# Expert blocks of 32 rows on four 32-column tiles, in an encoder layer with 32 experts on one core

## The reference

```
logits = x2 @ w_router + b_router
top_v, top_i = lax.top_k(logits, 4);  gates = softmax(top_v)
# for each expert e and the tokens that chose it:
gu = xb @ w_gate_up[e] + b_gate_up[e]          # 1024 -> 2048
gate = min(gu[:, :1024], 7);  up = clip(gu[:, 1024:], -7, 7)
hid = (up + 1) * gate * sigmoid(1.702 * gate)
y = hid @ w_down[e] + b_down[e]                # 1024 -> 1024
# the token's result: sum over its four experts of gate * y
```

## Time and profile before

| | before |
|---|---|
| median of 3 runs | 2055.57 us (2051.02 to 2067.83) |
| the profiled execution | 2061.79 us |
| its span | 2060.2 us |
| mean granted TensorE clock | 0.887 |
| TensorE busy | 1719.9 us, 83% |
| VectorE, ScalarE, GpSimd busy | 372.7, 337.3, 117.5 us |
| moved by DMA | 510.75 MB, mean 248 GB/s |

### The profile page before, as it was taken

One profiled execution on the slowest core, in us unless ns is written; L12 is line 12 of the kernel. 1 busy time (PEld: TensorE's weight loads), 2 busy tenths in 40 slices (PEclk: granted clock), 3 DMA queues, 4 the chain that ended last, 5 costly groups with the idle time before them and its releaser, 6 DMA issues.

```text
span 2060.2 us, 19415 instructions
## 1 busy us (share of the span) xinstructions
PE 1719.9 (83%) x7088; PEld 789.1 (38%) x7089; DVE 372.7 (18%) x899; ACT 337.3 (16%) x695; POOL 117.5 (6%) x219
## 2 busy tenths in 40 slices
PE   3999978688889998589877999979799987899890
PEld 1666544355556663333222333323233322233330
DVE  1371143322220011511010111101110111011113
ACT  1141254211221000111110111101111110111111
POOL 0021000000000000200000000000000000000003
PEclk9999976766669999599999999998999999999995
DMA  9396200110013344399999879999977999759894
GB/s 306 118 256 196 102 21 0 34 39 2 1 41 123 113 169 156 141 367 405 408 405 402 317 272 403 405 403 413 401 297 267 412 402 399 290 209 403 315 365 137
DMA packets 112324, 510.75 MB, mean 248 GB/s; under 512 B 8513, under 2 KB 12334, under 8 KB 79390
## 3 DMA queue, kind: packets, MB, share of 16 engines
q1 hardware_dynamic: 95790, 454.97, 56.4%
q0 software_dynamic: 16496, 55.29, 9.2%
HBM read 470.95 MB, written 39.28 MB: 248 GB/s over the span
## 4 chain that ended last, share of the span: by engine, by line
PE 65%; DMA 22%; DVE 6%; ACT 3%; issue 3%; SPq 1%; POOL 0%; DVEq 0%; POOLq 0%; ACTq 0%
PE bank L498 31%; DMA ring<-in_w_gate_up 18%; PE bank L826 12%; PE bank L851 10%; PE bank L834 7%; PE bank L502 2%; PE bank L817 2%; DVE r_c L1118 1%; DMA ring<-in_w_down 1%; ACT ring L878 1%; DMA ring<-in_w_in 1%; DVE r_v L1118 1%; DVE r_kv L1115 1%; ACT r_kv L878 1%; DMA y_rows<-r_xt 0%
## 5 line engine op out<-in xcount | busy, mean ns | idle before, releaser
L826 PE MATMUL bank<-ring,r_kv 128*64 128x512 f32 x1872 | 412.9, 593 | 27.2 <-DMA ring<-in_w_gate_up 27.2
L851 PE MATMUL bank<-ring,r_kv 128*64 128x512 f32 x1248 | 315.0, 662 | 27.8 <-ACT r_kv L878 26.8
L498 PE MATMUL bank<-r_xt,ring 128*128 128x336 f32 (+2 forms) x896 | 259.8, 453 | 8.6 <-DMA ring<-in_w_in 8.6
L826 PEld LDWEIGHTS bank<-ring,r_kv 128*64 128x64 f32 x1872 | 131.2, 137 | 302.6 <-issue 253.4
L1112 DVE TENSOR_SCALAR r_kv<-bank 128x512 f32<-128x512 f32 (+1 forms) x80 | 55.0, 687 | 1038.0 <-PE bank L834 1016.2
L498 PEld LDWEIGHTS bank<-r_xt,ring 128*128 128x128 f32 (+2 forms) x896 | 167.5, 188 | 99.1 <-issue 20.4
L834 PE MATMUL bank<-ring,r_kv 128*64 128x512 f32 x624 | 151.3, 630 | 39.9 <-DMA ring<-in_w_gate_up 39.9
L851 PEld LDWEIGHTS bank<-ring,r_kv 128*64 128x64 f32 x1248 | 94.7, 153 | 223.2 <-issue 181.5
L1070 ACT ACTIVATE r_o<-r_kv 128x512 f32<-128x512 f32 x39 | 24.6, 630 | 562.2 <-DVE r_kv L1112 562.2
L502 PE MATMUL bank<-const,r_v 64*128 64x64 f32 (+3 forms) x524 | 62.9, 258 | 60.0 <-DVE r_v L1118 49.3
L834 PEld LDWEIGHTS bank<-ring,r_kv 128*64 128x64 f32 x624 | 45.5, 144 | 141.6 <-issue 88.4
(11 more groups left out here) (212 smaller groups left out, 1092.7 us busy)
## 6 DMA issues: line engine op xcount, KB each, us to landing
ring<-in_w_gate_up SPq DMA_DIRECT2D x128, 2048.0 KB, 20.6
ring<-in_w_down SPq DMA_DIRECT2D x64, 2048.0 KB, 21.4
ring<-in_w_in SPq DMA_DIRECT2D x12, 2048.0 KB, 7.8
r_v<-x_rows POOLq DMA_DIRECT2D x40, 256.0 KB, 7.3
y_rows<-r_xt POOLq DMA_DIRECT2D x78, 128.0 KB, 5.5
x_rows<-r_c POOLq DMA_DIRECT2D x10, 768.0 KB, 18.4
x_rows<-r_c POOLq DMA_DIRECT2D x6, 1024.0 KB, 21.6
y_rows<-r_c POOLq DMA_DIRECT2D x1, 5376.0 KB, 33.1
```

Of the source, the lines that this page charges most:

```text
L498: ins = pe.matmul(out, l, r, start=(n == 0), stop=(n == len(pairs) - 1), **kw)
L826: ins = pe.matmul(half(gate_bank if q < 2 else up_bank, q % 2), xg[:, 2 * c + k, :], w[:, k, 512 * q:512 * q + 512], start=False, stop=Fal ...
L851: ins = pe.matmul(half(out_bank, t), hidT[:, j, BLK * c:BLK * c + BLK], w[:, j, 512 * t:512 * t + 512], start=(c == 0 and j == 0), stop=(c ...
```

## The change

`BLK` goes from 64 to 32, and everything of a block with it. The stationary operand has 32 columns, and four 32-column tiles of the array hold the same rows and produce a quarter of the output columns each, 256 per matmul; each PSUM bank holds 256 columns on 128 partitions. So gate and up are 64 matmuls of 256 columns instead of 32 of 512, down 32 instead of 16, the bias 8 instead of 4. The elementwise work of a block is on 128x256 instead of 128x512 elements, and `hid` is turned in two pieces instead of four.

The weights of an expert come in twelve transfers of 1 MiB (eight for gate and up, four for down) instead of six of 2 MiB; the last two of gate and up are waited for together. The down weights are grouped so that transfer j holds rows of both halves of the hidden dimension.

The turning of the next block's rows stays behind gate and up; the next block's bias matmuls move there too, behind a wait for the clamp of up (`m_read`). TensorE instead of ScalarE waits for `yrow_free`, ahead of the down product. GpSimd stores `yrow` in four pieces instead of two, and loads rows two blocks ahead instead of one.

The row buffers get MAXB = 74 blocks of 32 rows instead of 53 of 64; the tables for blocks grow from 55 to 76 entries, and the counting of blocks (`more`) has nine steps instead of four.

```diff
-NE, TOPK, BLK = 32, 4, 64
+NE, TOPK, BLK = 32, 4, 32
...
-        xg = r3(r_kv[:, 0:512], 8)
-        hidT = r3(r_kv[:, 512:1024], 4)
-        gt = r_kv[:, 1024:1536]
-        up = r_kv[:, 2048:2560]
-        sg = r_o[:, 0:512]
+        xg = r3(r_kv[:, 0:256], 8)
+        hidT = r3(r_kv[:, 512:768], 2)
+        gt = r_kv[:, 1024:1280]
+        up = r_kv[:, 2048:2304]
+        sg = r_o[:, 0:256]
         gateT = r_o[0:NE, 1024:1024 + NT]
-        hid = r_v[:, 0:512]
+        hid = r_v[:, 0:256]
         xrow = r_v[0:BLK, 1216:2240]
-        yrow = r_xt[:, 1280:1792]
-
-        def up_w(c):
-            return ring[:, UPSLOT[c] * SLOT:(UPSLOT[c] + 1) * SLOT].rearrange("p (k f) -> p k f", k=2)
-
-        def dn_w(c):
-            return ring[:, DNSLOT[c] * SLOT:(DNSLOT[c] + 1) * SLOT].rearrange("p (k f) -> p k f", k=4)
+        yrow = r_xt[:, 1280:1536]
+
+        def up_w(k):
+            at = UPSLOT[k // 2] * SLOT + 2 * D * (k % 2)
+            return ring[:, at:at + 2 * D]
+
+        def dn_w(j):
+            at = DNSLOT[j // 2] * SLOT + 2 * D * (j % 2)
+            return ring[:, at:at + 2 * D].rearrange("p (h f) -> p h f", h=2)
...
-            sp.dma_start(dn_w(0), dn[:, 0, 0:4, :]).then_inc(chunk_in[4], 16)
-            sp.dma_start(dn_w(1), dn[:, 0, 4:8, :]).then_inc(chunk_in[5], 16)
+            for j in range(4):
+                sp.dma_start(dn_w(j), dn[:, 0, :, j, :]).then_inc(dn_in[j], 16)
             sp.wait_ge(moe_tab, 1)
             with sp.Fori(1, NE) as e:
                 before = sp.value_load(firsti[0:1, bass.ds(e, 1)].bitcast(I32), min_val=0, max_val=MAXB)
-                for c in range(4):
-                    sp.wait_ge(m_up, before * 4 + c + 1)
-                    sp.dma_start(up_w(c), gu[:, bass.ds(e, 1), 2 * c:2 * c + 2, :].rearrange("p a k f -> p (a k) f")
-                                 ).then_inc(chunk_in[c], 16)
-                for c in range(2):
-                    sp.wait_ge(m_down, before * 2 + c + 1)
-                    sp.dma_start(dn_w(c), dn[:, bass.ds(e, 1), 4 * c:4 * c + 4, :].rearrange("p a k f -> p (a k) f")
-                                 ).then_inc(chunk_in[4 + c], 16)
+                for k in range(8):
+                    sp.wait_ge(m_up, before * 7 + min(k, 6) + 1)
+                    sp.dma_start(up_w(k), gu[:, bass.ds(e, 1), k, :].rearrange("p a f -> p (a f)")
+                                 ).then_inc(up_in[k], 16)
+                for j in range(4):
+                    sp.wait_ge(m_down, before * 4 + j + 1)
+                    sp.dma_start(dn_w(j), dn[:, bass.ds(e, 1), :, j, :].rearrange("p a h f -> p (a h) f")
+                                 ).then_inc(dn_in[j], 16)
...
+            def tile(bank, t):
+                return bank[BLK * t:BLK * t + BLK, 0:256]
+
+            def bias(b):
+
+                pe.wait_ge(m_pick, b + 1)
+                for q in range(8):
+                    pe.matmul(tile(gate_bank if q < 4 else up_bank, q % 4), pick[:, q // 2, :],
+                              bgu[:, 256 * (q % 2):256 * (q % 2) + 256], start=True, stop=False, skip_group_check=True)
+
+            bias(0)
             with pe.Fori(0, nb) as b:
                 e = pe.value_load(bei[0:1, bass.ds(b, 1)].bitcast(I32), min_val=0, max_val=NE - 1)
-
-                def half(bank, t):
-                    return bank[BLK * t:BLK * t + BLK, :]
-
-                pe.wait_ge(m_pick, b + 1)
-                for q in range(4):
-                    pe.matmul(half(gate_bank if q < 2 else up_bank, q % 2), pick[:, q, :], bgu[:, :],
-                              start=True, stop=False, skip_group_check=True)
                 pe.wait_ge(m_xg, b + 1)
-                for c in range(4):
-                    pe.wait_ge(chunk_in[c], 16 * e + 16)
-                    w = up_w(c)
-                    if c < 3:
-                        for k in range(2):
-                            for q in range(4):
-                                ins = pe.matmul(half(gate_bank if q < 2 else up_bank, q % 2), xg[:, 2 * c + k, :],
-                                                w[:, k, 512 * q:512 * q + 512], start=False, stop=False,
-                                                skip_group_check=True)
-                        ins.then_inc(m_up, 1)
-                    else:
-                        for bank_, q0, done in ((gate_bank, 0, m_gate), (up_bank, 2, m_up)):
-                            for k in range(2):
-                                for t in range(2):
-                                    ins = pe.matmul(half(bank_, t), xg[:, 2 * c + k, :],
-                                                    w[:, k, 512 * (q0 + t):512 * (q0 + t) + 512], start=False,
-                                                    stop=(k == 1), skip_group_check=True)
-                            ins.then_inc(done, 1)
+                for k in range(6):
+                    pe.wait_ge(up_in[k], 16 * e + 16)
+                    w = up_w(k)
+                    for q in range(8):
+                        ins = pe.matmul(tile(gate_bank if q < 4 else up_bank, q % 4), xg[:, k, :],
+                                        w[:, 256 * q:256 * q + 256], start=False, stop=False, skip_group_check=True)
+                    ins.then_inc(m_up, 1)
+                for k in (6, 7):
+                    pe.wait_ge(up_in[k], 16 * e + 16)
+                for bank_, q0, done in ((gate_bank, 0, m_gate), (up_bank, 4, m_up)):
+                    for k in (6, 7):
+                        for t in range(4):
+                            ins = pe.matmul(tile(bank_, t), xg[:, k, :],
+                                            up_w(k)[:, 256 * (q0 + t):256 * (q0 + t) + 256], start=False,
+                                            stop=(k == 7), skip_group_check=True)
+                    ins.then_inc(done, 1)
                 pe.wait_ge(m_xrow, 16 * b + 32)
                 pe.sem_inc(m_rows_in, 1)
                 tokens_turned()
+                pe.wait_ge(m_read, b + 1)
+                bias(b + 1)
                 pe.wait_ge(m_hid, b + 1)
-                for j in range(4):
+                for j in range(2):
                     ins = turn(ht_bank[:, 128 * j:128 * j + 128], hid[:, 128 * j:128 * j + 128])
                 ins.then_inc(m_turn, 1)
                 pe.wait_ge(m_hidT, b + 1)
-                for c in range(2):
-                    pe.wait_ge(chunk_in[4 + c], 16 * e + 16)
-                    w = dn_w(c)
-                    for j in range(4):
-                        for t in range(2):
-                            ins = pe.matmul(half(out_bank, t), hidT[:, j, BLK * c:BLK * c + BLK],
-                                            w[:, j, 512 * t:512 * t + 512], start=(c == 0 and j == 0),
-                                            stop=(c == 1 and j == 3), skip_group_check=True)
+                pe.wait_ge(yrow_free, b + 1)
+                for j in range(4):
+                    pe.wait_ge(dn_in[j], 16 * e + 16)
+                    w = dn_w(j)
+                    for h in range(2):
+                        s = 2 * h + j // 2
+                        for t in range(4):
+                            ins = pe.matmul(tile(out_bank, t), hidT[:, j % 2, BLK * s:BLK * s + BLK],
+                                            w[:, h, 256 * t:256 * t + 256], start=(j == 0 and h == 0),
+                                            stop=(j == 3 and h == 1), skip_group_check=True)
                     ins.then_inc(m_down, 1)
...
-                copy(hidT[:, :, :], banks[1][:, :].rearrange("p (j s) -> p j s", j=4)).then_inc(m_hidT, 1)
-                act.wait_ge(m_down, 2 * b + 2)
-                act.wait_ge(yrow_free, b + 1)
-                copy(yrow, banks[4][:, :]).then_inc(m_yrow, 1)
+                copy(hidT[:, :, :], banks[1][:, 0:256].rearrange("p (j s) -> p j s", j=2)).then_inc(m_hidT, 1)
+                act.wait_ge(m_down, 4 * b + 4)
+                copy(yrow, banks[4][:, 0:256]).then_inc(m_yrow, 1)
...
-                ts(gt, banks[2][:, :], LIMIT, ALU.min).then_inc(m_gt, 1)
+                ts(gt, banks[2][:, 0:256], LIMIT, ALU.min).then_inc(m_gt, 1)
                 ts(pick[:, :, :], lane, be[:, bass.ds(dve.snap(b + 1), 1)], ALU.is_equal).then_inc(m_pick, 1)
-                dve.wait_ge(m_up, 4 * b + 4)
-                ts(up, banks[3][:, :], LIMIT, ALU.min, -LIMIT, ALU.max).then_inc(m_dve, 1)
+                dve.wait_ge(m_up, 7 * b + 7)
+                ts(up, banks[3][:, 0:256], LIMIT, ALU.min, -LIMIT, ALU.max).then_inc(m_read, 1)
                 dve.wait_ge(m_sig, b + 1)
                 dve.wait_ge(m_gt, b + 1)
                 tt(gt, gt, sg, ALU.mult).then_inc(m_dve, 1)
-                dve.wait_ge(m_dve, 2 * b + 2)
+                dve.wait_ge(m_read, b + 1)
+                dve.wait_ge(m_dve, b + 1)
                 stt(hid, up, 1.0, gt, ALU.add, ALU.mult).then_inc(m_hid, 1)
...
+            pool.wait_ge(m_gath, 1)
+            pool.dma_start(xrow, x_rows_dram[BLK:2 * BLK, :]).then_inc(m_xrow, 16)
```

(37 more changed lines are left out.)

3 lines of the change are left out of this document (1 added, 2 removed).

## The result

The changed kernel takes 2130.21 us (median of 4 runs, 2127.78 to 2132.54) against 2056.35 us before (2051.02 to 2067.83): ratio 1.0351, 95% interval 1.0306 to 1.0397. It is slower by 74 us; the forecast was 2126 us, 70 slower. The profiled execution has a span of 2129.0 us.

A forecast was written before the change was run, and what follows sets the result against it. The prediction took the DMA queue to bound the loop: first request 877, stream 1005, holes 185 and tail 15 gave 2082 us against 2012, +70. The forecast was 2126 us, range 2078 to 2175.

The forecast's parts named there:

- first request: Start of the expert loop's weight loads: the first weight request stays at 877 us.
- holes: Expert loop: times without a weight request outstanding, behind experts with several blocks; 185 us in all instead of 106.
- a hole behind two blocks: Empty weight queue from an expert's last landing until its second block has used chunk 0; 4.4 us, before 10.9.
- an inner block: Each block beyond an expert's second, run with weights present while nothing is fetched; 13.7 us, before 27.6.
- stream without holes: Expert loop's weight and row transfers: 403.2 MB at 401 GB/s take 1005 us.
- tail behind the last landing: End of the loop: the last expert's second block comes wholly behind the last weight landing; 15 us.
- The DMA queue as the clock of the loop: Expert loop: time without a weight request is lost; faster TensorE gains only there and at the end.
- A block at four tiles: Block's matmuls: four tiles run beside each other, 54 ns an instruction; gate and up 6.9 us, down 3.5.
- yrow_free at TensorE: Down product's wait for the previous block's stores: ready after 8.7 us, needed after 9.2; at slowest landing 0.9 us.
- TensorE as the bound: Rival in the loop: four tiles no better than two, or lower clock; block 23.2 us, up to 2380 us; chance 0.05.
- Smaller transfers: Rival for weight loads: 186 added requests each cost 0.38 us, 71 us more, 2197 us; chance 0.02.
- A faster stream: Rival for weight loads: finer slots raise the rate; at 429 GB/s 2026 us; chance of faster 0.04, within 1% 0.07.

The follow-up runs named there:

- experiment 4: Changed kernel with 32 added float32 matmuls in each block, into PSUM banks that nobody reads; 2174.03 us, ratio 1.0572 to the kernel before.
- experiment 1: Changed kernel with blocks of 64 rows on two 64-column tiles, all else of the change kept; 2022.41 us, ratio 0.9829 to the kernel before.
- experiment 3: Changed kernel with six weight transfers of 2 MB instead of twelve of 1 MB, 32 rows kept; 2164.76 us, ratio 1.0517 to the kernel before.
- experiment 5: Kernel of experiment 1 with weight chunk 6 used when it lands, only chunk 7 waited for at the end; 2012.71 us, ratio 0.9770 to the kernel before.
- experiment 6: Kernel of experiment 1 with the bias matmuls put back to the start of the block; 2063.93 us, ratio 1.0029 to the kernel before.
- experiment 2: Kernel before with only the twelve 1 MB weight transfers instead of six of 2 MB; 2057.94 us, ratio 0.9989 to the kernel before.
- experiment 8: Kernel of experiment 1 with six weight transfers of 2 MB instead of twelve; 2028.29 us, ratio 0.9838 to the kernel before.
- experiment 7: Changed kernel, 32 rows, with weight chunk 6 used when it lands and only chunk 7 waited for; 2134.90 us, ratio 1.0368 to the kernel before.
- experiment 9: Changed kernel, 32 rows, with the bias matmuls put back to the start of the block; 2148.49 us, ratio 1.0429 to the kernel before.

## Why the prediction was right

By its own steps, predicted and measured:

| term | predicted | measured |
|---|---|---|
| first request | 877 | 875.0 |
| holes | 185 | 179 |
| a hole behind two blocks | 4.4 (at full clock 2.8) | 4.1 to 4.6 |
| an inner block | 13.7 (at full clock 12.7) | 13.2 to 13.3 |
| stream without holes | 1005 | 1007 (last weights at 2061.7) |
| tail behind the last landing | 15 | 16 |
| loop ends | 2082 | 2077.8 |
| behind the last down product, more than before | 1 | 3 |

- **Blocks.** 58, as reckoned: the page of the changed kernel counts 232 stores of rows, four for each block. Experts with one block follow each other every 31.0 to 31.3 us, where 31 to 32 were forecast.
- **The DMA queue as the clock of the loop.** Shown by experiment 4 (203 us of matmuls cost 44) and by experiments 1, 3, 5 and 6, in which the time moves with the sum of the holes: 75, 222, 61 and 106 us of holes, 2022, 2165, 2013 and 2064 us. Experiment 2 doesn't speak against it: its holes didn't shrink either. The eleven profiles cut into four parts say the same (us; "stream" is the time from the first to the last weight packet of the loop, less the holes):

| kernel | first packet | stream | holes | behind the last packet | span |
|---|---|---|---|---|---|
| before, 64 rows | 879 | 1019 | 106 | 56 | 2060 |
| experiment 1 | 873 | 1021 | 75 | 53 | 2022 |
| experiment 2 | 880 | 1017 | 107 | 61 | 2065 |
| experiment 5 | 877 | 1022 | 61 | 51 | 2011 |
| experiment 6 | 871 | 1017 | 106 | 60 | 2054 |
| experiment 8 | 885 | 1017 | 79 | 52 | 2032 |
| changed, 32 rows | 876 | 1006 | 179 | 67 | 2129 |
| experiment 3 | 876 | 1003 | 222 | 69 | 2170 |
| experiment 4 | 868 | 1011 | 218 | 72 | 2169 |
| experiment 7 | 876 | 1007 | 183 | 66 | 2132 |
| experiment 9 | 866 | 1003 | 205 | 69 | 2142 |

The stream is the same within 5 us at 64 rows and within 8 us at 32, whatever TensorE does; the holes range over 161 us.

- **A block at four tiles.** 54 ns an instruction, as taken, and not the 75 of the earlier trace rows. The lower clock was there where it was expected (0.73 between holes, 0.83 over the loop). One number that hung on it was wrong: TensorE is busy 912 us in the loop and not under 750. In the stretch between holes shown above an instruction takes 83 ns of busy time in the mean, in the hole behind three blocks 58. In the changed kernel that cost nothing: the clock is 1.00 in all of its holes.
- **Luck in two terms.** The hole and the inner block were each taken between a sum at full clock and one at the lower clock. The lower clock didn't come in any hole, and the sums at full clock were short: by 1.3 us or more in a hole, by 0.6 in a block. In the hole at 1193.08, for one, 0.5 us pass from the last packet to the first down matmul and 0.3 from the last one to the next block, which the sum leaves out, and some 1.4 instead of 1.0 from chunk 0 to the next packet. The allowance for a clock that didn't come stood in for these. By its own sums at full clock the holes would have been 17 x 2.8 + 8 x 12.7 = 149 us and the forecast 2090: still slower and still in the range, but 40 us under what was measured.
- **Moved bias.** The prediction called it free and gave it no gain. With 32 rows it is worth 18 us (experiment 9), with 64 rows 41 (experiment 6). The sum held it, since the block of 12.7 us was reckoned with it hidden and the new hole without it, but no line gave it a worth, and the clock behind the wait for hid was seen only as a cost. With 32 rows it isn't quite free either: from up to down 2.5 us pass with it and 2.3 without.
- **yrow_free at TensorE.** "It just fits": no wait of TensorE for a store is among its waits in the loop. What the rows loaded two blocks ahead are worth was not tried by itself.
- **Rivals.** TensorE as the bound: excluded by experiment 4 for 32 rows. With 64 rows it is half true: in experiment 6 TensorE's block does lengthen the loop, through the holes. Smaller transfers: excluded by experiment 3, and by experiment 2, which has the 186 added requests and none of the 71 us. With them falls, for a queue that is kept filled, the use of the figure for 1 MB that the Trainium skill gives on its page DMA: Bandwidth & Descriptors, section Bandwidth (341 GB/s): here 406 GB/s were moved in transfers of 1 MB. A faster stream: 400 GB/s outside the holes, before and after.
- The page TensorEngine Tiling (Array Packing) of the Trainium skill, section Theoretical Speedup, allows up to 4 times for 32 columns; the trace agrees for matmuls of 256 columns as far as four against two tiles go (four in 0.216 us, a pair of 512 columns in 0.43), and the loop shows that it isn't the time that counts.

## What to carry to other kernels

Where one queue feeds a loop, add up the times in which nothing can be requested, before the work of the engines: a smaller block that makes each step twice as fast also makes more steps that hold the buffers, and only the last step of a group lets the next transfers go. Take the parts of such a change apart: here the block size lost 108 us, while at the old block size the rest of the change, with the weights used as they land, brought 46 us over the kernel before, and in experiment 6, without the moved bias, the rest brought nothing. And try independent matmuls in a wait in the middle of a block: here they kept the clock up for what follows.

## What the runs showed that was not expected

- **The clock took back a shorter step.** In experiment 2, at the hole shown, a wait of 4.6 instead of 3.1 us ahead of the last chunks went with 6.39 instead of 3.68 us for the same 16 instructions, and 9.98 instead of 7.09 for the down product. With the bias in the gap the granted clock over the loop goes with that wait: 1.00 where it is 0.6 us (experiment 5) or 1.3 us (experiment 8), 0.97 where it is 3.1 us (experiment 1). Nothing was tried that changes the wait alone.
- **A wait of 3.4 us with 1.9 us of bias matmuls in it** left the down product at 7.09 us in all 39 blocks of experiment 1; without them it took 8.4 to 10.1 us in 29 of the 39 (experiment 6). The other ten follow last chunks that had to be waited for.
- **SyncE's requests take longer when many transfers are outstanding.** In the changed kernel a request takes at most 0.38 us while up to six transfers of 1 MB haven't landed, and up to 5.4 us with seven to ten of them. In the kernel before, 0.37 us is the median with up to four of 2 MB outstanding, and 2.3 us (9.2 at most) with five. The requests of down weights take 0.37 us at least, 1.3 in the median, where those of the kernel before had a median of 0.37. In the chain of the changed kernel requests stand for 6% of the span:

```profile
L488 SPq DMA_DIRECT2D ring<-in_w_down x124: 372/1312/5419, 884.9 to 2039.5; - x124
```

The queue kept 406 GB/s meanwhile, so it isn't a loss. The chain probably names the request because it was the last thing ahead of a transfer that had to wait its turn anyway; no run tests that.
